# A streaming encoder layer: the vector engine prepares the second chunk of queries of a head earlier

## The reference, cut to what matters

```
def step(s, inp):                       # one block of frames
    q_i, k_i, v_i, lf_i = inp           # lf = log f
    b = jnp.cumsum(lf_i, axis=1)
    inter = jnp.einsum('bthd,bhde->bthe', q_i * jnp.exp(b), s)
    diff = b[:, :, None] - b[:, None, :]
    diff = jnp.where(tri[None, :, :, None, None], diff, -jnp.inf)
    att = jnp.einsum('bthd,btshd->bhts', q_i, jnp.exp(diff) * k_i[:, None])
    intra = jnp.einsum('bhts,bshe->bthe', att, v_i)
    b_last = b[:, -1]
    k_dec = k_i * jnp.exp(b_last[:, None] - b)
    s_new = jnp.exp(b_last)[..., None] * s + jnp.einsum('bshd,bshe->bhde', k_dec, v_i)
    return s_new, inter + intra
```

## Time and profile before

| | us |
|---|---|
| median of 3 executions | 2508.93 |
| lowest, highest | 2507.73, 2509.86 |
| the profiled execution | 2509.86 |
| its span, from first to last instruction | 2508.1 |
| PE busy | 2463.8 |
| DVE busy | 1149.9 |
| ACT busy | 672.3 |
| POOL busy | 483.8 |

### The profile page before, as it was taken

How to read it: one execution, slowest core, us unless ns; L and a number is a source line. 1 busy time by engine, 2 the same in 40 slices (tenths; PEclk the granted TensorE clock), 3 DMA queues, 4 the chain that set the end, 5 groups by cost and what they waited for, 6 DMA issues and landing times.

```text
span 2508.1 us, 37476 instructions
## 1 busy us (share of the span) xinstructions
PE 2463.8 (98%) x14264; PEld 2345.4 (94%) x14264; DVE 1149.9 (46%) x2297; ACT 672.3 (27%) x1365; POOL 483.8 (19%) x729
## 2 busy tenths in 40 slices
PE   6999999999999999999999999999999999999998
PEld 6999999999999999999999999888899899898996
DVE  4052524324276667557665444455333343343335
ACT  5132232323222222222222332233122031131121
POOL 1020211102164456436544000001000000000000
PEclk9999999999999999999999999999999999999999
DMA  4251535344333323423432634222011021120114
GB/s 152 89 196 65 195 108 174 123 154 148 105 120 125 120 76 124 138 91 103 134 115 90 218 126 132 87 91 84 26 51 50 17 67 33 33 62 30 42 42 159
DMA packets 219183, 256.88 MB, mean 102 GB/s; under 512 B 8257, under 2 KB 186817, under 8 KB 218945
## 3 DMA queue, kind: packets, MB, share of 16 engines
q1 hardware_dynamic: 219072, 255.37, 30.9%
HBM read 175.12 MB, written 80.22 MB: 102 GB/s over the span
## 4 chain that ended last, share of the span: by engine, by line
PE 78%; issue 11%; DVE 5%; DMA 2%; POOL 2%; ACT 1%; SPq 1%; POOLq 0%; DVEq 0%; ACTq 0%
PE bank L596 12%; PE bank L598 11%; PE bank L597 11%; PE bank L826 5%; PE bank L827 5%; PE bank L828 5%; PE bank L897 5%; PE bank L896 5%; PE bank L895 5%; PE bank L747 3%; PE bank L856 1%; PE bank L854 1%; PE bank L855 1%; DMA ZQ<-scratch_z 1%; POOL ORS L1609 1%
## 5 line engine op out<-in xcount | busy, mean ns | idle before, releaser
L596 PE MATMUL bank<-XH,WHI 128*128 128x384 f32 x2304 | 789.8, 343 | 8.6 <-DVE XL L1242 4.3
L598 PE MATMUL bank<-XH,WLO 128*128 128x384 f32 x2304 | 774.0, 336 | 0.0
L597 PE MATMUL bank<-XL,WHI 128*128 128x384 f32 x2304 | 773.3, 336 | 0.0
L596 PEld LDWEIGHTS bank<-XH,WHI 128*128 128x128 f32 x2304 | 435.2, 189 | 14.0 <-ACT XH L911 6.2
L597 PEld LDWEIGHTS bank<-XL,WHI 128*128 128x128 f32 x2304 | 435.3, 189 | 0.9
L598 PEld LDWEIGHTS bank<-XH,WLO 128*128 128x128 f32 x2304 | 434.7, 189 | 0.0
L911 ACT ACTIVATE ZST<-bank 128x384 f32<-128x384 f32 x240 | 117.7, 491 | 546.1 <-PE bank L598 544.1
L826 PE MATMUL bank<-XH,WHI 128*128 128x384 f32 x768 | 257.7, 336 | 3.6 <-ACT XH L911 3.6
L827 PE MATMUL bank<-XL,WHI 128*128 128x384 f32 x768 | 257.4, 335 | 0.0
L828 PE MATMUL bank<-XH,WLO 128*128 128x384 f32 x768 | 257.4, 335 | 0.0
L1212 DVE TENSOR_TENSOR WLO<-WRAW,WHI 128x1024 fp32r<-128x1024 f32 x128 | 160.1, 1251 | 209.7 <-ACT WHI L911 205.3
(11 more groups left out here) (173 smaller groups left out, 3198.1 us busy)
## 6 DMA issues: line engine op xcount, KB each, us to landing
scratch_z<-ZST SPq DMA_DIRECT2D x80, 576.0 KB, 3.0
WRAW<-in_w_in SPq DMA_DIRECT2D x80, 512.0 KB, 3.9
HZ<-scratch_z SPq DMA_DIRECT2D x32, 576.0 KB, 5.0
WRAW<-in_w_up SPq DMA_DIRECT2D x32, 512.0 KB, 4.0
WRAW<-in_w_down SPq DMA_DIRECT2D x32, 512.0 KB, 3.3
MG<-scratch_z SPq DMA_DIRECT2D x16, 576.0 KB, 5.8
ZQ<-scratch_z SPq DMA_DIRECT2D x4, 1152.0 KB, 6.5
ZK<-scratch_z SPq DMA_DIRECT2D x4, 1152.0 KB, 8.5
```

Source lines behind the costliest of these rows:

```text
L596: pe.matmul(psum[c][:, 0:CH], WHI[p][:, k, :], XH[:, k, s], start=(k == 0), stop=False)
L597: pe.matmul(psum[c][:, 0:CH], WHI[p][:, k, :], XL[:, k, s], start=False, stop=False)
L598: last = pe.matmul(psum[c][:, 0:CH], WLO[p][:, k, :], XH[:, k, s], start=False, stop=(k == KT - 1))
```

## The change

In slots 0 and 1 the vector engine now makes part 0 and part 1 of chunk 1. Before, part 0 stood in slot 1 and part 1 behind the mean of tile 0, at the end of slot 4. Chunk 2 (slots 6 and 7) stays as it is: `s % 6` gives 0 and 1 there as well.

```
@@ -1431,10 +1431,10 @@
                         n = 40 + 10 * i + jj
                         if c == 0 and jj:
                             wlo_block(n + 1, (jj + 1) % 2)
-                        if s in (1, 6, 7):
+                        if s in (0, 1, 6, 7):
                             if s == 6:
                                 dve.wait_ge(H.sc, 9 * h + 3)
-                            prep_q(h, 1 + s // 6, 0 if s < 7 else 1)
+                            prep_q(h, 1 + s // 6, s % 6)
                         if s >= HA and s - HA < NT:
                             weights(h, s - HA)
                         if HA + 2 <= s < HA + 2 + NT:
@@ -1460,8 +1460,6 @@
...
                             head_ms(H, h, t, HD)
-                            if t == 0:
-                                prep_q(h, 1, 1)
                         if s >= HG_SLOTS - 2 and not end:
                             if s == HG_SLOTS - 2:
                                 forget(h + 1)
```

## The result

| | before | after |
|---|---|---|
| median, 6 runs each | 2508.12 us | 2532.95 us |
| lowest, highest | 2506.86, 2509.86 | 2528.14, 2538.85 |
| ratio of the times, 95% interval | | 1.0101 (1.0086 to 1.0115) |
| profiled execution, span | 2509.86, 2508.1 | 2537.56, 2535.8 |

The changed kernel is 24.8 us slower, 1.0%. Its times also scatter more: 10.7 us from lowest to highest, against 3.0 before.

A forecast was written before the change was run, and what follows sets the result against it. PE, busy 98% of the span, was taken to bound the kernel. 20.6 us of new waits plus 3.3 us of half clock made 23.9 us, so a median of 2533 us, 1.0% slower, range 2518 to 2549.

The forecast's parts named there:

- the removal: Taking the nine part 1 instructions from slot 4's end: worth nothing; 5.7 us of idle PE bounds any gain.
- moving part 0: Part 0 of chunk 1 from slot 1 to slot 0: starts when it did before, costs nothing.
- The deadline: PE stops before slot 4's transposes until tile 0's weights are made; slack 2.0 us in head 2.
- X: Length of the nine moved instructions in their new place beside GpSimd's keys: 5.62 us, from chunk 0's same nine.
- Y: Vector engine time from the nine's place to the end of tile 0's weights, weight block included: 3.61 us.
- the two rivals built on X: No contention beside GpSimd: X 3.27, 2512 us, chance 0.11. Strict turns on the shared port: X 8.58, 2566 us, chance 0.07.
- 8.58: Upper bound of X in us: each of the nine held up once by a whole GpSimd instruction of 0.59 us.
- 3.27: Lower bound of X in us: the nine in head 4's old place, with GpSimd's keys out of the way.
- Waits of 20.6 us: PE's eight new waits before slot 4's attention, one per head, 1.09 to 3.63 us, longest in heads 2 and 4.
- The distances to the deadline: From part 0's end to PE's need of tile 0's weights, per head: 5.60 to 8.14 us, subtracted from 9.23.
- Half clock: 3.3 us: Lower PE clock behind the waits of heads 2 and 4: two stretches of some 3.4 us; bounds none or 13.1 us.
- Sum: Whole loss: 20.6 us of waits plus 3.3 of half clock, 23.9 us, giving a median of 2533 us.

The follow-up runs named there:

- e7: Changed kernel with slot 3's weight block behind tile 0's weights and GpSimd's chunk 1 keys held until chunk 1's queries are ready: 2508.94 us, ratio 0.9997.
- e3: Changed kernel with GpSimd's keys of chunk 1 held until chunk 1's queries are ready, its gate products ahead of that wait: 2513.35 us, ratio 1.0015.
- e8: The changed kernel run once more, unaltered, for a second profile: 2532.35 us, ratio 1.0089.
- e1: Kernel before, with part 1 of chunk 1 directly behind tile 0's weights in slot 3 instead of at the end of slot 4: 2510.92 us, ratio 1.0008.
- e4: Kernel before, with ten fills of a spare tile on the vector engine ahead of tile 0's weights in slot 3: 2534.10 us, ratio 1.0109.
- e6: Kernel before, with six fills of a spare tile on the vector engine ahead of tile 0's weights in slot 3: 2510.77 us, ratio 1.0004.
- e5: Kernel before, with forget(0), the decays of head 0, ahead of the weight block of line 1480 instead of behind it: 2508.43 us, ratio 0.9996.

## Why the prediction was right, point by point

- *PE bounds the stage; the removal wins nothing; moving part 0 costs nothing.* Right. e7 shows no gain with the nine instructions early and the waits gone.
- *The deadline is slot 4's transposes, for tile 0's weights.* Right: eight waits at line 738 for line 1401, and none elsewhere.
- *X = 5.62 us, Y = 3.61.* In head 2 after: 5.61 (889.12 to 894.73) and 3.39 (to 898.12). Over all heads the nine took 5.0 to 5.9 us. The choice of the earlier trace rows over the earlier trace rows was right, and e3 shows the reason. Of the two rivals built on X, neither bound was met: 8.58 was too high and 3.27 too low. The Trainium skill's "SBUF — State Buffer", section "Who interferes with whom", names these two engines' shared read port. That they slow each other, the trace bears out (e3). The 8.58 us was my own reading of that rule, a whole GpSimd instruction of delay for each of the nine, and in head 2 two of them took 0.36 and 0.37 us, as when left alone. Whether the port is held for a whole instruction, no run here decides.
- *Waits of 20.6 us.* Too high by 6.0; that heads 2 and 4 would wait longest held for head 2 alone. Heads 1, 3 and 5 were near (2.06 against 2.25), and so was head 0 in the first profile (2.58 against 2.63). The distances to the deadline were off in heads 2, 4, 6 and 7. Heads 2 and 4 begin behind a turn of the loop, where the start of part 0 differs from run to run (head 2 of the changed kernel: 2.22 and 1.77 us idle ahead of part 0, and waits of 3.13 and 2.71, in two profiles). In head 4 I took 3.63 and it was 1.75. In head 7 I took 2.87 from a part 0 that lasted 4.86 us; in the kernel after it lasted 3.72, and the wait was 0.44. One profile's length for each head was treated as fixed, where only that of heads 1, 3 and 5 is.
- *Half clock: 3.3 us.* This step failed. It said of the waits: "2.87 and less I count as too short". Waits of 2.58, 2.06, 2.06 and 1.75 us were followed by the lower clock, and three of the stretches lasted 6.8 us, not 3.4. It cost 13.6 us, four times the term and above even its upper bound of 13.1, which gave every stretch 3.4 us. It was a threshold read from two long waits and a few under 1.3 us, with nothing in between.
- *Sum.* 23.9 forecast, 24.8 measured. That it is so near is luck. Between the two profiled executions the waits were 6.0 us less than forecast, the clock cost 10.3 more, 2.3 more went elsewhere in the stage (1.5 for the evacuation and 0.8 not broken down), and 2.9 were gained ahead of it: 27.6, against 27.7 between the spans. The median lies 3 us under that, since the profiled execution after lies 4.6 us above its own median and the one before 1.7 above its. The range was wide enough for either.

## What to carry to other kernels

When work is moved earlier on an engine that isn't the bottleneck, look for the next thing that the bottleneck takes from that engine, and count from there; a list that is half idle on average can have as little as 2 us of slack at one place. Size moved instructions by a row that runs beside the same neighbour, not by their fastest row. And price a new wait of PE twice, as its own length and as the clock behind it, with the second price a chance rather than a threshold.

## What the hardware showed that I had not expected

Over seven profiles of kernels that delay tile 0's weights (after, e8, e1 to e4 and e6), PE waited 40 times for them. None of the 26 waits of 1.40 us or less was followed by the lower clock level; of the 14 between 1.75 and 3.13 us, ten were. Of five waits of 2.06 us two were followed by it and three not, and over the ten a stretch lasted 3.4 or 6.8 us. Its length isn't fixed even for one and the same wait: near the end of that for head 0's keys, 3.28 to 3.41 us in nine of the ten profiles, a low stretch began each time, three times of 3.4 us and six times of 6.8. Outside this set, in e5, a wait of 1.44 us for another engine was followed by one as well, so 1.40 is no safe bound. What decides between two equal waits stays open.
